# A triangular inverse on stored 64x64 diagonal chunks, each in its own corner of the array

## The chip, the cores and the metric

The kernel runs on one core of a Trainium2 chip. The metric is the device time of the whole program in microseconds. Before the change the median of three runs is 1731.29 us (1727.56 to 1732.21).

## The reference, cut to what matters

The program computes two transformer-like blocks for 256 tokens of width 1024. Only one of the four branches of the first block's mixer is touched, `rwkv7_scan`:

```python
def step(s, inp):                       # for each head, N = 64, T = 256 tokens
    r_t, w_t, k_t, v_t, a_t, b_t = inp
    sa = einsum('bhvk,bhk->bhv', s, a_t)
    s = s * w_t + sa[..., None] * b_t + v_t[..., None] * k_t
    return s, einsum('bhvk,bhk->bhv', s, r_t)
```

The kernel doesn't step through the tokens. It takes chunks of 64 tokens; within a chunk the steps depend on each other through a strictly triangular 64x64 matrix A of products of a_t and b_t, and what is needed is the inverse of (I - A), applied to the rest. There are four heads and four chunks, so 16 such matrices.

## The kernel before

The stage is one `nc.Block()` in which each engine runs its own written-out list, ordered by semaphores. Its parts, in TensorE's order from L866 on:

- **Pair products** (L870 to L879). A pair of heads' rows and a pair of chunks is one index m of 8: `pair(m)` gives the head, its channel block c, the partition half p (0 or 64, set by `odd = m // 4`) and the token block tt of 128 tokens. For each m, five kinds of 128x128 products of the scaled vectors (a·b, b·a, k·a, b·r, k·r) are made from 64 partitions each; all kinds of `odd = 0` come first, then those of `odd = 1`. Four m fill a PSUM bank; ten banks' worth go through six banks, so the later ones wait for `pair_read`. A 128x128 product spans two chunks, of which only the two diagonal 64x64 blocks are used: DVE's masks (`level0`, `levels_t`, `upper`, `upper_eq`) put zeros elsewhere.
- DVE (L666 to L683) masks them into X, XT (the inverse as built so far and its transpose), MT, MTak, MTrb, MTrk, each 8 matrices of 128x128.
- **Levels** (L881 to L899, five of them, `LEVELS`). Each doubles the size of the inverted diagonal blocks. NT is MT masked for the level (DVE, L689). TensorE makes Z = NT·X (L888), ACT copies it out of PSUM (L770, L771), TensorE makes the two products of Z with XT (L896, L897; in the last level only L897), and DVE's `grow` (L566 to L573) adds them to X and XT.
- **Gate products** (`gate_products`, L231 with `channels`): projections of the mixer's gates, with no relation to the inverse, 128x256 moving, 8 weights each, which TensorE does between the steps while DVE or ACT work. Their weights come over SP's queue through four ring slots; ACT reads the results (L542).
- **After the levels**: the MTak products (L903), DVE's copy (L695), G and H (L910), ACT's copy (L778, L779), then the products within a chunk (L918 to L920), the products per chunk (L928 to L930), a walk over the four chunks (L938, L943), and a group norm (L947, L950).

`turn` (L517) makes TensorE wait for its own last product where it goes from one half of the array's rows to the other on the same banks. Every f32 product shows as two weight loads and two matmuls in the profile.

Of the kernel before, what the change touches and what calls it, by code (L numbers as in the profile page):

```python
# [12 lines left out]
P = 128  # L13
T = 256
# [29 lines left out]
FIRST = {"lora": 512, "ln_rows": 512, "sgw": 512, "sgb": 512, "same": P, "upper": P, "upper_eq": P,  # L44
         "level0": P, "levels_t": 6 * P, "after": P, "causal": P, "sb_mask0": T, "sb_mask1": P, "carry": T,
         "eye2": 64}
# [58 lines left out]
def build(nc, out, stream, x_t, meta_t, cols, first, second, last, keep):  # L105
    with ExitStack() as ctx:
        sems = {}

        def S(name):

            if name not in sems:
                sems[name] = ctx.enter_context(nc.semaphore(name))
            return sems[name]
# [215 lines left out]
        def f(name, n=None):  # L329
            return fst[:, f_at[name]:f_at[name] + (n or FIRST[name])]  # L330
# [164 lines left out]
        X, XT, Z, NT, MT, MTak, MTrb, MTrk = (a2.take(8, P) for _ in range(8))  # L495
# [10 lines left out]
        rp, y0, yd2, state, sc_c, sc_t = X[:, 0:4, :], X[:, 4:8, :], Z[:, 0:4, :], NT[:, 0, :], y[:, 6:8, :], Z  # L506
        rp, y0, yd2 = (v.rearrange("p a b -> p (a b)").rearrange("p (c t) -> p c t", c=2) for v in (rp, y0, yd2))
# [15 lines left out]
        def four(m):  # L523
            return m.unsqueeze(1).broadcast_to([P, 4, m.shape[1]])

        def eight(m):
            return m.unsqueeze(1).broadcast_to([P, 8, m.shape[1]])

        def b3(b, w=T):

            return bank[b][:, :].rearrange("p (c t) -> p c t", t=w)
# [14 lines left out]
        with nc.Block() as block:  # L546
# [19 lines left out]
            def grow(dve, v, lev):  # L566
                dve.wait_ge(S("level_x"), lev)
                for half in range(2):
                    q4 = slice(4 * half, 4 * half + 4)
                    if lev < LEVELS:  # L570
                        vec.link(v.tensor_tensor(X[:, q4, :], X[:, q4, :], b3(4 + half, P), ALU.add))
                    ins = v.tensor_tensor(XT[:, q4, :], XT[:, q4, :], b3(6 + half, P), ALU.add)
                    vec.link(ins) if half == 0 else vec.tell(ins, S("level_grown"), lev)  # L573

            @block.vector
            def _(dve):
# [88 lines left out]
                n = 0  # L665
                lv = f("levels_t").rearrange("p (l t) -> p l t", l=6)  # L666
                for odd in range(2):
                    q4 = slice(4 * odd, 4 * odd + 4)
                    for kind in range(5):
                        b = 2 + n % 6  # L670
                        dve.wait_ge(S("pair_done"), n + 1)
                        src = b3(b, P)
                        if kind == 0:
                            vec.tell(v.tensor_tensor(X[:, q4, :], src, four(f("level0")), ALU.mult), S("pair_read"), n + 1)
                            vec.link(v.tensor_tensor(X[:, q4, :], X[:, q4, :], four(ident), ALU.add))
                        elif kind == 1:
                            vec.tell(v.tensor_copy(MT[:, q4, :], src), S("pair_read"), n + 1)
                            vec.link(v.tensor_tensor(XT[:, q4, :], MT[:, q4, :], four(lv[:, 0, :]), ALU.mult))
                            vec.link(v.tensor_tensor(XT[:, q4, :], XT[:, q4, :], four(ident), ALU.add))
                        else:  # L680
                            dst, m = ((MTak, "upper"), (MTrb, "upper_eq"), (MTrk, "upper_eq"))[kind - 2]
                            vec.tell(v.tensor_tensor(dst[:, q4, :], src, four(f(m)), ALU.mult), S("pair_read"), n + 1)
                        n += 1  # L683


                for lev in range(1, LEVELS + 1):
                    if lev > 1:
                        dve.wait_ge(S("level_z"), lev - 1)
                    vec.tell(v.tensor_tensor(NT, MT, eight(lv[:, lev, :]), ALU.mult), S("level_nt"), lev)  # L689
                    if lev > 1:  # L690
                        grow(dve, v, lev - 1)
# [37 lines left out]
            def _(act):  # L729
# [58 lines left out]
            def _(pe):  # L788
# [79 lines left out]
                n = 0  # L868
                for odd in range(2):
                    for lhs, rhs in ((a_t, b_t), (b_t, a_t), (k_t, a_t), (b_t, r_t), (k_t, r_t)):  # L870
                        if n >= 6:
                            pe.wait_ge(S("pair_read"), n - 5)
                        for m in range(4):
                            _, c, p, tt = pair(4 * odd + m)
                            o = slice(tt * P, (tt + 1) * P)
                            ins = mm(bank[2 + n % 6][:, m * P:(m + 1) * P], lhs[p:p + 64, c, o], rhs[p:p + 64, c, o],
                                     start=True, stop=True)
                        ins.then_inc(S("pair_done"), 1)
                        n += 1  # L879
                gate_products(pe, 1)  # L880
                for lev in range(1, LEVELS + 1):  # L881
                    pe.wait_ge(S("level_nt"), lev)
                    if lev == 1:
                        pe.wait_ge(S("pair_read"), 10)
# [7 lines left out]
                    pe.wait_ge(S("level_zc"), lev)  # L892
                    for m in range(8):
# [5 lines left out]
                    gate_products(pe, 1)  # L899

                for m in range(8):
                    hh, _, _, tt = pair(m)
                    ins = mm(bank[2][:, m * 64:(m + 1) * 64], MTak[:, m, :],  # L903
                             tm[:, 3, tt, hh * 64:(hh + 1) * 64], start=True, stop=True)
# [4 lines left out]
                for m in range(8):  # L909
                    ins = mm(bank[3 + m // 4][:, m % 4 * P:(m % 4 + 1) * P], XT[:, m, :], AM[:, m, :],  # L910
                             start=True, stop=True)
# [3 lines left out]
                for m in range(8):  # L915
                    hh, c, p, tt = pair(m)
                    o = slice(c * T + tt * P, c * T + (tt + 1) * P)
                    mm(bank[5][p:p + 64, o], GH[:, m, 0:64], MTrb[:, m, :], start=True, stop=True)  # L918
                    mm(bank[6][p:p + 64, o], GH[:, m, 64:P], MTrb[:, m, :], start=True, stop=False)
                    mm(bank[6][p:p + 64, o], tm[:, 3, tt, hh * 64:(hh + 1) * 64], MTrk[:, m, :], start=False, stop=True)  # L920
# [1806 lines left out]
def lay_out(a):  # L2727
# [73 lines left out]
    masks += levels[:1] + [m.T for m in levels]  # L2801
    masks += [s_ > t_, s_ <= t_, s_ < t2, s_ < t2[:, P:] - P, (t2 % 64 != 0) & (s_ >= 0)]
    eye2 = np.concatenate([np.eye(64), np.eye(64)], 0)
    first = [lora, ln_rows, sgw, sgb.reshape(P, 512)] + [m.astype(f32) for m in masks] + [eye2]
# [45 lines left out]
```

## Time and profile before

| | before |
|---|---|
| median of runs | 1731.29 us |
| profiled execution, its own time | 1728.11 us |
| its span | 1726.3 us |
| TensorE busy | 1657.2 us (96%) |
| DVE busy | 1151.3 us (67%) |
| ACT busy | 795.1 us (46%) |
| TensorE's mean granted clock | 0.984 |

The chain that ended last covers only the final few microseconds, so the profile is read by stretches. In the table of stretches and in the timeline, PE is TensorE's matmuls, PEld its weight loads. A matmul's record includes the latency from its start to its results, so consecutive records overlap; spacing is taken from starts.

### The profile page before, as it was taken

How to read it: one execution, taken by the hardware profiler on the slowest of the kernel's cores; microseconds unless marked ns; L12 is line 12 of the kernel's file. 1: busy time of each engine (PE TensorE's matmuls, PEld its weight loads, DVE VectorE, ACT ScalarE, POOL GpSimd, SP SyncE). 2: the span in 40 equal slices, each digit the busy share in tenths (PEclk: the TensorE clock that was granted, in tenths of full speed). 3: DMA queues.
4: the chain of work that ended last, by engine and by line, in shares of the span. 5: the costliest groups of instructions: out<-in, count | busy, mean ns of one | idle time of the engine just before them, and what ended most of it. 6: DMA issues, size and time to landing. Idle time of an engine off the chain costs nothing. (4 is left out here: it accounts for less than half of the span.)

```text
span 1726.3 us, 32696 instructions
## 1 busy us (share of the span) xinstructions
PE 1657.2 (96%) x11202; PEld 1508.7 (87%) x11202; DVE 1151.3 (67%) x2276; ACT 795.1 (46%) x1318; POOL 354.3 (21%) x225
## 2 busy tenths in 40 slices
PE   7999998979999999999999998999999999999997
PEld 7988897869999977778999998999999888888886
DVE  6473414667777584662779994777776577777776
ACT  5251112245554363223455554455555555555554
POOL 1030000014443001335767995000000000000000
PEclk9999998989999999999999999999999999999999
DMA  7423223335555521115545786555556877777773
GB/s 280 146 61 110 74 86 135 99 125 188 186 183 185 181 64 50 49 47 184 196 150 188 219 228 182 181 178 171 178 172 199 240 239 237 235 235 241 242 238 127
DMA packets 92806, 289.47 MB, mean 168 GB/s; under 512 B 10304, under 2 KB 27072, under 8 KB 92352
## 3 DMA queue, kind: packets, MB, share of 16 engines
q1 hardware_dynamic: 92304, 287.61, 51.8%
q10 hardware_dynamic: 432, 0.90, 0.2%
q8 instruction: 47, 0.77, 0.2%
q14 instruction: 23, 0.19, 0.0%
HBM read 270.64 MB, written 17.83 MB: 167 GB/s over the span
## 5 line engine op out<-in xcount | busy, mean ns | idle before, releaser
L260 PE MATMUL psum<-arena_parts 128*128 128x256 f32 (+2 forms) x1664 | 478.9, 288 | 24.9 <-DVE ring_parts L255 11.8
L262 PE MATMUL psum<-arena_parts,ring_parts 128*128 128x256 f32 (+1 forms) x1600 | 450.8, 282 | 0.0
L2638 DVE TENSOR_TENSOR ring_parts<-ring,arena_parts 128x512 fp32r<-128x512 f32 x418 | 282.6, 689 | 113.2 <-ACT arena_parts L2438 94.5
L260 PEld LDWEIGHTS psum<-arena_parts 128*128 128x128 f32 x1664 | 316.0, 190 | 27.8 <-DVE ring_parts L255 10.9
L262 PEld LDWEIGHTS psum<-arena_parts,ring_parts 128*128 128x128 f32 x1600 | 304.2, 190 | 0.0
L261 PE MATMUL psum<-h_parts,arena_parts 128*128 128x256 f32 x1024 | 290.2, 283 | 0.0
L255 POOL TENSOR_TENSOR ring_parts<-ring,arena_parts 128x1024 fp32r<-128x1024 f32 x79 | 211.0, 2695 | 64.7 <-ACT arena_parts L251 47.8
L231 PE MATMUL psum<-h,ring 128*128 128x256 f32 x896 | 210.4, 394 | 0.0
L2407 PE MATMUL psum<-arena_parts,x_parts 128*128 128x512 f32 x512 | 198.8, 388 | 2.7 <-DVE x_parts L2665 2.7
L2409 PE MATMUL psum<-arena_parts,x_parts 128*128 128x512 f32 x512 | 201.2, 393 | 0.0
L2408 PE MATMUL psum<-ring_parts,x_parts 128*128 128x512 f32 x512 | 200.9, 392 | 0.0
L231 PEld LDWEIGHTS psum<-h,ring 128*128 128x128 f32 x896 | 174.6, 198 | 28.5 <-issue 3.2
L261 PEld LDWEIGHTS psum<-h_parts,arena_parts 128*128 128x128 f32 x1024 | 194.1, 190 | 0.0
L2438 ACT ACTIVATE arena_parts<-ring 128x512 fp32r<-128x512 f32 x209 | 131.5, 629 | 112.0 <-PE psum L2409 93.1
L261 PE MATMUL psum<-arena_parts 128*128 128x256 f32 (+1 forms) x576 | 163.6, 284 | 0.0
L2435 ACT ACTIVATE arena_parts<-ring 128x512 fp32r<-128x512 f32 x209 | 131.8, 631 | 67.1 <-PE psum L2409 55.4
L1108 DVE TENSOR_TENSOR ring_parts<-ring,arena_parts 128x1024 fp32r<-128x1024 f32 x66 | 84.3, 1284 | 52.8 <-ACT arena_parts L1103 48.2
L2407 PEld LDWEIGHTS psum<-arena_parts,x_parts 128*128 128x128 f32 x512 | 96.1, 188 | 24.8 <-DVE ring_parts L2638 2.9
L2408 PEld LDWEIGHTS psum<-ring_parts,x_parts 128*128 128x128 f32 x512 | 96.1, 188 | 22.0
L2409 PEld LDWEIGHTS psum<-arena_parts,x_parts 128*128 128x128 f32 x512 | 96.3, 188 | 19.1
L261 PEld LDWEIGHTS psum<-arena_parts 128*128 128x128 f32 x576 | 110.0, 191 | 0.2
L251 ACT ACTIVATE arena_parts<-ring 128x1024 fp32r<-128x1024 f32 x76 | 78.6, 1053 | 60.3 <-DMA ring<-stream 60.3
(540 smaller groups left out, 2952.9 us busy)
## 6 DMA issues: line engine op xcount, KB each, us to landing
ring<-stream SPq DMA_DIRECT2D x473, 512.0 KB, 3.6
kept<-arena SPq DMA_DIRECT2D x128, 128.0 KB, 2.0
arena<-kept SPq DMA_DIRECT2D x32, 512.0 KB, 4.1
arena<-first SPq DMA_DIRECT2D x1, 2144.0 KB, 16.5
arena<-second SPq DMA_DIRECT2D x1, 1632.0 KB, 6.4
x<-x_t SPq DMA_DIRECT2D x1, 1024.0 KB, 5.6
out<-arena SPq DMA_DIRECT2D x4, 256.0 KB, 2.1
arena<-last ACTq DMA_DIRECT2D x1, 512.0 KB, 3.5
```

Source lines behind the costliest of these rows:

```text
L231: mm = nc.tensor.matmul(b[:, 0:width], w[:, k, :], h[:, k, lo:lo + width], start=k == 0, stop=k == KT - 1)
L255: ns.tensor_tensor(low[:, s, :], ring[:, s, :], high[:, s, :].bitcast(F32), ALU.subtract)\
L260: nc.tensor.matmul(dst, stationary[0], moving[0], start=first, stop=False)
L261: nc.tensor.matmul(dst, stationary[0], moving[1], start=False, stop=False)
L262: return nc.tensor.matmul(dst, stationary[1], moving[0], start=False, stop=last_one)
L1108: nc.vector.tensor_tensor(low[:, s, :], ring[:, s, :], high[:, s, :].bitcast(F32), ALU.subtract)\
L2407: mm(b, gate_high[:, q % 4, t], expert_high[:, m % 2, w], start=False, stop=False)
L2408: mm(b, gate_high[:, q % 4, t], low[:, s, w], start=False, stop=False)
L2409: ins = mm(b, gate_low[:, q % 4, t], expert_high[:, m % 2, w], start=False, stop=last_one)
L2435: nc.scalar.activation(expert_high[:, m % 2, halves[0]], ring[:, s, halves[0]], ACT.Copy)\
L2438: nc.scalar.activation(expert_high[:, m % 2, halves[1]], ring[:, s, halves[1]], ACT.Copy)\
L2638: v.tensor_tensor(low[:, s, w], ring[:, s, w], expert_high[:, m % 2, w].bitcast(F32), ALU.subtract)\
```

## The change

X, XT, Z, NT, MT, MTak, MTrb and MTrk are stored as 8 matrices of 64 columns: partitions 0 to 63 hold the first chunk's 64x64 block, 64 to 127 the second's. All masks are stacked in the same way on the host, with a zero pad so that `first` has its old size. Each 128x128 product of the inverse becomes two 64x64 products, one from and to rows 0 to 63, the other from and to rows 64 to 127. The pair products run in the order kind, m, chunk r, `odd`, so that successive ones alternate the row halves; they fit in six banks at once, and DVE reads two banks in one operation. The X and XT additions, NT and the copy of Z are one operation of 512 elements per partition each. The products within a chunk (`within`) alternate the two heads' column halves, and are done for one row half at a time, before the chunk products of the same half. y0 has its own place. Added waits: `pair_read` 4 before the first product with Z, `pair_read` 6 before the MTak products.

```diff
-        X, XT, Z, NT, MT, MTak, MTrb, MTrk = (a2.take(8, P) for _ in range(8))
+        X, XT, Z, NT, MT, MTak, MTrb, MTrk = (a2.take(8, CH) for _ in range(8))
+        y0 = a2.take(2, T)
...
-                for half in range(2):
-                    q4 = slice(4 * half, 4 * half + 4)
-                    if lev < LEVELS:
-                        vec.link(v.tensor_tensor(X[:, q4, :], X[:, q4, :], b3(4 + half, P), ALU.add))
-                    ins = v.tensor_tensor(XT[:, q4, :], XT[:, q4, :], b3(6 + half, P), ALU.add)
-                    vec.link(ins) if half == 0 else vec.tell(ins, S("level_grown"), lev)
+                if lev < LEVELS:
+                    vec.link(v.tensor_tensor(X, X, b3(3, CH), ALU.add))
+                vec.tell(v.tensor_tensor(XT, XT, b3(7, CH), ALU.add), S("level_grown"), lev)
...
+                dve.wait_ge(S("pair_done"), 1)
+                vec.tell(v.tensor_tensor(by_half(X), pairs_of(2, 0), each(f("level0")), ALU.mult), S("pair_read"), 1)
+                vec.tell(v.tensor_copy(by_half(MT), pairs_of(2, 1)), S("pair_read"), 2)
+                vec.link(v.tensor_tensor(X, X, eight(f("eye2")), ALU.add))
+                vec.tell(v.tensor_tensor(NT, MT, eight(lv[:, 1, :]), ALU.mult), S("level_nt"), 1)
+                vec.link(v.tensor_tensor(XT, MT, eight(lv[:, 0, :]), ALU.mult))
+                vec.tell(v.tensor_tensor(XT, XT, eight(f("eye2")), ALU.add), S("pair_read"), 3)
+                for kind, (dst, b, half, m) in enumerate(((MTrk, 6, 0, "upper_eq"), (MTak, 4, 0, "upper"), (MTrb, 4, 1, "upper_eq"))):
+                    dve.wait_ge(S("pair_done"), 3)
+                    vec.tell(v.tensor_tensor(by_half(dst), pairs_of(b, half), each(f(m)), ALU.mult), S("pair_read"), 4 + kind)
...
-                    a.activation(Z[:, 0:4, :], b3(2, P), ACT.Copy)
-                    sca.tell(a.activation(Z[:, 4:8, :], b3(3, P), ACT.Copy), S("level_zc"), lev)
+                    sca.tell(a.activation(Z, b3(2, CH), ACT.Copy), S("level_zc"), lev)
...
+                for kind, (lhs, rhs) in enumerate(((a_t, b_t), (b_t, a_t), (k_t, a_t), (b_t, r_t), (k_t, r_t))):
+                    for m in range(4):
+                        for r in range(2):
+                            for odd in range(2):
+                                _, c, p, tt = pair(4 * odd + m)
+                                o = slice(tt * P + CH * r, tt * P + CH * (r + 1))
+                                at_m = kind % 2 * T + m * CH
+                                ins = mm(bank[2 + kind // 2 * 2 + odd][chunk_rows[r], at_m:at_m + CH],
+                                         lhs[p:p + 64, c, o], rhs[p:p + 64, c, o], start=True, stop=True)
+                    if kind % 2 or kind == 4:
                         ins.then_inc(S("pair_done"), 1)
...
                     for m in range(8):
-                        ins = mm(bank[2 + m // 4][:, m % 4 * P:(m % 4 + 1) * P], NT[:, m, :], X[:, m, :],
-                                 start=True, stop=True)
+                        for r in chunk_rows:
+                            ins = mm(bank[2][r, m * CH:(m + 1) * CH], NT[r, m, :], X[r, m, :], start=True, stop=True)
...
                     for m in range(8):
-                        o = slice(m % 4 * P, (m % 4 + 1) * P)
+                        o = slice(m * CH, (m + 1) * CH)
                         if lev < LEVELS:
-                            mm(bank[4 + m // 4][:, o], XT[:, m, :], Z[:, m, :], start=True, stop=True)
-                        ins = mm(bank[6 + m // 4][:, o], Z[:, m, :], XT[:, m, :], start=True, stop=True)
+                            for r in chunk_rows:
+                                mm(bank[3][r, o], XT[r, m, :], Z[r, m, :], start=True, stop=True)
+                        for r in chunk_rows:
+                            ins = mm(bank[7][r, o], Z[r, m, :], XT[r, m, :], start=True, stop=True)
...
                 for m in range(8):
-                    ins = mm(bank[3 + m // 4][:, m % 4 * P:(m % 4 + 1) * P], XT[:, m, :], AM[:, m, :],
-                             start=True, stop=True)
+                    for r in chunk_rows:
+                        ins = mm(bank[3 + m // 4][r, m % 4 * P:(m % 4 + 1) * P], XT[r, m, :], AM[r, m, :],
+                                 start=True, stop=True)
...
+                def within(r):
+                    for m in range(4):
+                        two_heads = [(4 * odd + m, *pair(4 * odd + m)) for odd in range(2)]
+                        for j, hh, c, p, tt in two_heads:
+                            o = slice(c * T + tt * P + r.start, c * T + tt * P + r.stop)
+                            mm(bank[5][p:p + 64, o], GH[r, j, 0:64], MTrb[r, j, :], start=True, stop=True)
...
                 for ch in (0, 2, 1, 3):
                     if ch == 1:
                         turn(pe, ins)
+                    if ch < 2:
+                        within(chunk_rows[ch])
```

## Rows read from the trace of the kernel before

**Rows 1.** The page: the span, and engines' busy time with its share of the span.

```profile
span 1726.3 us, 32696 instructions
PE 1657.2 (96%) x11202; PEld 1508.7 (87%) x11202; DVE 1151.3 (67%) x2276; ACT 795.1 (46%) x1318; POOL 354.3 (21%) x225
```

**Rows 2.** Stretches: us; PE, PEld, DVE, ACT, POOL busy (instructions); clock, DMA share, GB/s.

```profile
165.89:174.68 8.79, 8.79 (x82) 8.67 (x81) 7.18 (x11) 0.47 (x1) 0.00 (x0) 1.00 0.18 60
174.68:180.04 5.36, 3.72 (x17) 2.96 (x16) 5.10 (x7) 0.47 (x1) 0.00 (x0) 1.00 0.10 9
180.04:192.20 12.16, 12.16 (x80) 11.36 (x81) 3.97 (x5) 1.56 (x3) 0.00 (x0) 1.00 0.25 84
192.20:204.47 12.27, 12.27 (x82) 11.44 (x81) 3.97 (x5) 2.04 (x4) 0.00 (x0) 1.00 0.30 87
...
229.00:239.48 10.48, 10.48 (x66) 9.65 (x65) 1.37 (x2) 2.04 (x4) 0.00 (x0) 1.00 0.28 102
239.48:244.24 4.76, 3.86 (x34) 3.73 (x33) 0.69 (x1) 1.08 (x3) 0.00 (x0) 1.00 0.35 110
...
251.35:256.35 5.00, 5.00 (x49) 4.83 (x48) 0.00 (x0) 0.47 (x1) 0.00 (x0) 1.00 0.33 108
256.35:259.90 3.55, 3.49 (x98) 3.29 (x97) 0.00 (x0) 0.00 (x0) 0.00 (x0) 1.00 0.00 0
...
270.45:290.45 20.00, 14.88 (x77) 10.13 (x77) 10.05 (x14) 3.55 (x6) 0.00 (x0) 0.74 0.06 26
```

**Rows 3.** Timeline, pair stage: start, us, engine, line, operation, tiles, count [idle before].

```profile
165.89 8.86 PE L876 MATMUL psum<-arena 64*128 64x128 f32 x80
...
167.16 0.69 DVE L674 TENSOR_TENSOR arena<-psum,arena 128x512 f32<-128x512 f32 x1 [24.06 <-PE psum L876]
...
176.59 2.14 DVE L682 TENSOR_TENSOR arena<-psum,arena 128x512 f32<-128x512 f32 x3
...
178.76 1.23 DVE L689 TENSOR_TENSOR arena<-arena 128x1024 f32<-128x1024 f32 x1
...
180.04 2.05 PE L888 MATMUL psum<-arena 128*128 128x128 f32 x16 [1.64 <-DVE arena L689]
```

**Rows 4.** Timeline of one level, the second.

```profile
192.41 1.95 PE L888 MATMUL psum<-arena 128*128 128x128 f32 x16
...
194.20 3.62 PE L231 MATMUL psum<-h,ring 128*128 128x256 f32 x16
...
203.66 0.69 DVE L572 TENSOR_TENSOR arena<-arena,psum 128x512 f32<-128x512 f32 x1
```

**Rows 5.** Timeline, the walk over chunks: products on the two diagonal corners.

```profile
270.45 0.31 PEld L938 LDWEIGHTS psum<-arena 64*64 64x64 f32 x8 [0.33 <-issue]
...
270.74 0.40 PE L943 MATMUL psum<-arena 64*64 64x64 f32 x8
```

**Rows 6.** Timeline: the second half of the chunk products, and the column-halved L844.

```profile
136.89 1.15 PE L844 MATMUL psum<-arena 128*64 128x128 f32 x16
...
258.19 0.19 PEld L928 LDWEIGHTS psum<-arena 64*64 64x64 f32 x2 [0.20 <-PE psum L930]
...
259.69 0.28 PE L930 MATMUL psum<-arena 64*64 64x64 f32 x2
```

**Rows 7.** Timeline of L815 to L817, where the tile's size changes.

```profile
113.17 0.18 PEld L815 LDWEIGHTS psum<-arena 64*128 64x128 f32 x1 [0.33 <-issue]
...
113.49 0.38 PE L815 MATMUL psum<-arena 64*128 64x256 f32 x1
...
113.80 0.30 PEld L817 LDWEIGHTS psum<-arena 128*128 128x128 f32 x2 [0.33 <-issue]
```

**Rows 8.** Timeline after the levels: MTak products, copy, G and H, gate products.

```profile
239.69 1.89 PE L903 MATMUL psum<-arena 128*128 128x64 f32 x16
...
241.69 0.69 DVE L695 COPY arena<-psum 128x512 f32<-128x512 f32 x1 [3.78 <-PE psum L903]
242.49 2.02 PE L910 MATMUL psum<-arena 128*128 128x128 f32 x16 [0.90 <-issue]
...
244.35 7.07 PE L231 MATMUL psum<-h,ring 128*128 128x256 f32 x32
```

More of the change, by code:

```diff
@@ L42 @@
         "ssm_log_dt_2": 16, "ml_b_if_2": 2}
-FIRST = {"lora": 512, "ln_rows": 512, "sgw": 512, "sgb": 512, "same": P, "upper": P, "upper_eq": P,
-         "level0": P, "levels_t": 6 * P, "after": P, "causal": P, "sb_mask0": T, "sb_mask1": P, "carry": T,
-         "eye2": 64}
+CH = 64
+FIRST = {"lora": 512, "ln_rows": 512, "sgw": 512, "sgb": 512, "same": P, "upper": CH, "upper_eq": CH,
+         "level0": CH, "levels_t": 6 * CH, "after": P, "causal": P, "sb_mask0": T, "sb_mask1": P, "carry": T,
+         "eye2": 64, "unused": 9 * CH}
 SECOND = {"b_re": 512, "b_im": 512, "c_re": 512, "c_im": 512, "w_if": 192, "neg0": T, "neg1": T, "sel": 512}
@@ L527, in eight, with pairs_of, by_half, each @@
             return m.unsqueeze(1).broadcast_to([P, 8, m.shape[1]])
+        def pairs_of(b, kind):
+            two = psum[:, b * 512:(b + 2) * 512].rearrange("p (o x) -> p o x", o=2)
+            return two[:, :, kind * T:(kind + 1) * T].rearrange("p o (m k) -> p o m k", k=CH)
+        def by_half(m):
+            return m.rearrange("p (o m) k -> p o m k", o=2)
+        def each(m):
+            return m.unsqueeze(1).unsqueeze(1).broadcast_to([P, 2, 4, CH])
         def b3(b, w=T):
@@ L662, in _ @@
                 vec.tell(v.tensor_copy(y[:, 2:4, :], b3(3)), S("early_read"))
-                n = 0
                 lv = f("levels_t").rearrange("p (l t) -> p l t", l=6)
[L667 to L683, printed above, removed]
@@ new lines, in _ @@
+                vec.link(v.tensor_tensor(XT, MT, eight(lv[:, 0, :]), ALU.mult))
[3 more added lines that the diff above has]
+                    vec.tell(v.tensor_tensor(by_half(dst), pairs_of(b, half), each(f(m)), ALU.mult), S("pair_read"), 4 + kind)
+                for lev in range(2, LEVELS + 1):
+                    dve.wait_ge(S("level_z"), lev - 1)
@@ L867, in _ @@
                 pe.wait_ge(S("tm_read"), 1)
[L868 to L876, printed above, removed]
-                                     start=True, stop=True)
+                chunk_rows = [slice(CH * r, CH * (r + 1)) for r in range(2)]
+                for kind, (lhs, rhs) in enumerate(((a_t, b_t), (b_t, a_t), (k_t, a_t), (b_t, r_t), (k_t, r_t))):
[8 more added lines that the diff above has]
+                    if kind % 2 or kind == 4:
                         ins.then_inc(S("pair_done"), 1)
-                        n += 1
                 gate_products(pe, 1)
@@ L883, in _ @@
                     if lev == 1:
-                        pe.wait_ge(S("pair_read"), 10)
+                        pe.wait_ge(S("pair_read"), 2)
                     else:
@@ L892, in _ @@
                     pe.wait_ge(S("level_zc"), lev)
+                    if lev == 1:
+                        pe.wait_ge(S("pair_read"), 4)
                     for m in range(8):
-                        o = slice(m % 4 * P, (m % 4 + 1) * P)
+                        o = slice(m * CH, (m + 1) * CH)
                         if lev < LEVELS:
-                            mm(bank[4 + m // 4][:, o], XT[:, m, :], Z[:, m, :], start=True, stop=True)
-                        ins = mm(bank[6 + m // 4][:, o], Z[:, m, :], XT[:, m, :], start=True, stop=True)
+                            for r in chunk_rows:
+                                mm(bank[3][r, o], XT[r, m, :], Z[r, m, :], start=True, stop=True)
+                        for r in chunk_rows:
+                            ins = mm(bank[7][r, o], Z[r, m, :], XT[r, m, :], start=True, stop=True)
                     ins.then_inc(S("level_x"), 1)
                     gate_products(pe, 1)
+                pe.wait_ge(S("pair_read"), 6)
                 for m in range(8):
                     hh, _, _, tt = pair(m)
-                    ins = mm(bank[2][:, m * 64:(m + 1) * 64], MTak[:, m, :],
-                             tm[:, 3, tt, hh * 64:(hh + 1) * 64], start=True, stop=True)
+                    for r in chunk_rows:
+                        ins = mm(bank[2][r, m * 64:(m + 1) * 64], MTak[r, m, :],
+                                 tm[r, 3, tt, hh * 64:(hh + 1) * 64], start=True, stop=True)
                 ins.then_inc(S("mv_done"), 1)
@@ L909, in _ @@
                 for m in range(8):
-                    ins = mm(bank[3 + m // 4][:, m % 4 * P:(m % 4 + 1) * P], XT[:, m, :], AM[:, m, :],
-                             start=True, stop=True)
+                    for r in chunk_rows:
+                        ins = mm(bank[3 + m // 4][r, m % 4 * P:(m % 4 + 1) * P], XT[r, m, :], AM[r, m, :],
+                                 start=True, stop=True)
                 ins.then_inc(S("gh_done"), 1)
@@ L914, in _ @@
                 pe.wait_ge(S("gh_read"), 1)
[L915 to L920, printed above, removed]
+                def within(r):
[4 more added lines that the diff above has]
+                            mm(bank[5][p:p + 64, o], GH[r, j, 0:64], MTrb[r, j, :], start=True, stop=True)
+                        for j, hh, c, p, tt in two_heads:
+                            o = slice(c * T + tt * P + r.start, c * T + tt * P + r.stop)
+                            mm(bank[6][p:p + 64, o], GH[r, j, 64:P], MTrb[r, j, :], start=True, stop=False)
+                        for j, hh, c, p, tt in two_heads:
+                            o = slice(c * T + tt * P + r.start, c * T + tt * P + r.stop)
+                            mm(bank[6][p:p + 64, o], tm[r, 3, tt, hh * 64:(hh + 1) * 64], MTrk[r, j, :], start=False, stop=True)
                 for ch in (0, 2, 1, 3):
@@ L2801, in lay_out @@
     masks += levels[:1] + [m.T for m in levels]
+    masks[1:] = [np.concatenate([m[:CH, :CH], m[CH:, CH:]], 0) for m in masks[1:]]
     masks += [s_ > t_, s_ <= t_, s_ < t2, s_ < t2[:, P:] - P, (t2 % 64 != 0) & (s_ >= 0)]
     eye2 = np.concatenate([np.eye(64), np.eye(64)], 0)
-    first = [lora, ln_rows, sgw, sgb.reshape(P, 512)] + [m.astype(f32) for m in masks] + [eye2]
+    first = [lora, ln_rows, sgw, sgb.reshape(P, 512)] + [m.astype(f32) for m in masks] + [eye2, np.zeros((P, 9 * CH))]
     first = np.concatenate([x.astype(f32, copy=False) for x in first], 1)
```

10 lines of the change are left out of this document (3 added, 7 removed).

## The prediction

> **What bounds the kernel now.** I read the page first: TensorE is busy for 1657.2 of the span's 1726.3 us, 96%, and every other engine is far below it [rows 1]. That says where to look, not what this change is worth, so the next view is the table of stretches, cut at the starts of the stage's pieces [rows 2]. The changed code runs from 165.89 us (the pair products) to 259.90 us (the last chunk product). In the four rounds of the levels, and in the products of L918 to L920, TensorE has no idle time at all; it waits only in 174.68 to 180.04 (busy 3.72 of 5.36 us) and in 239.48 to 244.24 (3.86 of 4.76). DVE has 4 of 12.27 us of work in a level, ACT 2, and DMA is below 0.36 of its capacity in all these stretches. So here time is what TensorE has to stream, plus two waits for DVE.
>
> The third view is the timeline. In the pair stage TensorE is done by 174.7, but DVE's 16 masking operations, started at 167.16, end at 178.7 (0.72 us each), then comes NT (1.23 us), and the first level starts only at 180.04 [rows 3]. In a level the order is products of NT and X, a gate product, products with Z, a gate product. DVE's last addition ends at 204.35, when the second gate product is just being finished [rows 4]: the two engines are balanced, with TensorE ahead by nothing.
>
> A word on units. Each f32 product is two passes (a weight load and a matmul each); "pass" below is one of them. A full 128x128 pass with 128 moving columns takes 0.112 us (16 of L888 take 1.79 us, from 192.41 to 194.20 [rows 4]). A gate product takes 3.45 us: 32 passes last 7.07 us and 16 last 3.62 [rows 4, 8], the difference. Check: 2 x 3.45 + 48 x 0.112 = 12.28, and a level lasts 12.27 [rows 2].
>
> **The pace of 64x64 passes.** The change makes two passes on a 64x64 tile out of each 128x128 pass, the two in different corners of the array. It pays only if corners run at the same time. The nearest rows are L938 and L943, whose tiles are just these two diagonal corners, and which write the two row halves of one PSUM bank, as the new levels do: 16 passes, weights from 270.45, last matmul record until 271.14, which holds about 0.1 us of first load and 0.17 us of latency (a 256-column record lasts 0.38 us for 0.21 us of columns [rows 7]). That leaves 0.42 us for 16, 0.026 us each [rows 5]. L928 to L930 alternate two corners of one row half: from 258.29 to 259.80, 48 passes, 0.031 us each, and over the whole stretch with its turn 3.55/98 = 0.036 [rows 2, 6]. I take 0.028 and keep 0.026 and 0.031 as ends. With 128 moving columns on two corners I take 0.056, since L844 (two column halves) does 16 in 1.15 us, 0.058 apart [rows 6].
>
> **The price of changing the tile's size.** From L815 (64x128) to L817 (128x128) and between them the records show it: weights of L815 at 113.17, of L817 at 113.80, 0.63 us for two passes of 256 columns, which need 0.43 [rows 7]. (L816 runs beside them on the other row half.) So each change of size costs 0.2 us. Before, a level has none; after it has four, 0.84 us with rounding upward. Bounds: 0.1 (the weight load alone) and 0.33 us (the idle time that the profile gives the load queue there).
>
> **Part by part.**
> Pair products: 80 passes become 160, and now all four corners are used in turn. At 0.028 they take 4.5 us; no row shows four corners at once, so the bounds are 0.015 (twice two corners) and 0.031, that is 2.4 and 5.0 us. I stay at the two-corner pace, the nearest row. The Trainium skill ("TensorE: Matmul & The Clock Gate", its section on the clock's levels and floors) says that matmuls never start less than about 25 ns apart, however few the columns; by that rule the four corners would give 4.0 us and not 2.4. No row here has a burst under 0.026, which agrees. DVE now gets its first data after 64 passes, not 8; 165.99 + 1.8 + 0.3 = 168.1 (0.3 as today, from 8 x 0.108 past 165.99 to 167.16), and needs four operations before level 1 may start (X masked, MT, X plus identity, NT, each 512 wide, 4 x 0.72): 171.0. TensorE does its passes until 170.5, changes size (0.2), does a gate product (3.45), changes again (0.2): 174.35. The gate product thus covers DVE by 3.3 us; were it absent, level 1 would wait for DVE until 171.0. Today's first matmul of level 1 is at 180.04 plus 0.1 of load. Gain 5.8 us (5.3 to 7.9). The remaining five DVE operations end at about 174.7, and the added wait (MTrk read before the first Z product, because bank 7 is reused) ends at 173.2; the Z product is due at 174.35 + 0.9 + 3.85 = 179.1, so nothing queued behind it on TensorE is held.
>
> Levels 1 to 4: 2 x 3.45 + 96 x 0.028 + 0.84 = 10.43 against 12.27 (12.16 in the first). Gain 4 x 1.84 - 0.1 = 7.25 us (6.1 with 0.031, 10 with 0.026 and 0.1 us switches). DVE's part shrinks with it: NT 1.23 to 0.69, four additions to two, so 1.45 us after a Z product, under the 3.45 of the gate product; ACT's copy of Z is one operation, not two. Neither becomes late. Level 5 has no product for X: 6.9 + 64 x 0.028 + 0.84 = 9.53 against 10.48, gain 0.95.
>
> MTak products and G/H: today 4.66 us from the first matmul at 239.69 to the gate's at 244.35. Of this 2.0 are passes until DVE's copy starts at 241.69, 0.8 the copy and the wait for it (L910 at 242.49), 1.86 the L910 passes [rows 8]. After: 0.2 + 0.9 + 0.2 + 0.8 + 32 x 0.056 + 0.2 = 4.1. Gain 0.5: the wait stays, and 128 moving columns on two corners only break even.
>
> L918 to L920: 48 passes of a 128x64 tile with 128 columns take 5.0 us, because the two column halves stand in two long blocks. They become 96 alternating passes, 2.7 us plus 0.1; the switch to 64x64 before L928 goes too. Gain 2.2 us (1.9 to 2.4). The moved turn between row halves costs its 0.2 us once as before.
>
> The rest has one answer: the `first` transfer keeps its size by a zero pad, y0 gets a place of its own, the masks are the same elements stacked. The loads on SP's queue wait for the slots as before and only come some us earlier; DMA has room [rows 2]. After 259.90 the stage ends with an alternation of DVE and TensorE, and then a block boundary at which all engines meet, so the gain is passed on whole.
>
> Sum: 5.8 + 7.25 + 0.95 + 0.5 + 2.2 = 16.7 us, within 14 to 21. The profiled execution is 1728.11 us (span 1726.3), so it would come to 1711.4; the median of the runs, 1731.29, to **1714.6 us**. A measurement of this kernel tells about 0.3% (5.2 us) from no change.
>
> **The rivals.**
> (a) Corners of different row halves do not run together when they write the same bank. Then a 64x64 pass costs 0.056 (half of 0.112, since L903, with 64 moving columns but full weights, is no faster than 0.118 and so is bound by the weight's columns [rows 8]). A level takes 6.9 + 5.4 + 0.84 = 13.1, a loss of 3.5 over four; level 5 loses 0.85; MTak and G/H (3.6 for the latter) 2.1; pairs (a bank for each row half) and L918 (one row half at a time) keep their 8.0. Net gain 1.5 us: 1729.8, no change. The Trainium skill ("TensorEngine Tiling (Array Packing)", on PSUM pressure) states just this rule. Against it stand L938 and L943, which are two row halves on one bank at 0.026. Chance 6%.
> (b) The clock. TensorE's granted clock is 1.00 through the whole stage and falls to a mean of 0.74 in 270.45 to 290.45, where it waits again and again [rows 2]. If short passes on half the array drew the 1.2 GHz level in turns, at the same mean 0.74, the 66 us from the pairs to the second gate product after G/H would take 89, 23 more: 6.5 us slower than today, 1737.8. It decides from a mean clock of 66/(66+16.7) = 0.80 downward. Against it: the clock is 1.00 in 256.35 to 259.90, which is 64x64 passes alone. Chance 4%.
> (c) The passes come slower, at the 0.036 of the whole L928 stretch, because TensorE has to be fed 768 more instructions. Pairs then gain 4.5, levels 4.2, level 5 0.4, the next 0.2, L918 1.4: 10.7 us, 1720.6. Chance 12%.
> (d) Four corners at once and cheaper switches: 20 us, 1711. Chance 13%.
> That the change does not do what it says shows as a level with 48 passes; the text of the diff leaves no room for it.
>
> **How the numbers follow.** The forecast (gain 14 to 19) has 65%. Range: from 1705 (the best bounds, 21 us, plus some 4 us of spread between runs and of where the clock falls in the 20 us after the stage) to 1723 (case c, and 2.5 us of spread). It leaves out (a), (b) and little else, some 15%. Chances: faster by over 0.3%: 0.89; same: 0.07; slower: 0.04.
>
> **What would show it.** A level's period of 10.4 us (12.3 would show the 0.028 or the switches wrong); z bursts of 32 passes in 0.9 us; level 1 starting 8.4 us after the first pair product instead of 14.1, with no idle time before it; L918 to L920 in 2.7 us; granted clock 1.00 up to G/H; the stage from the first pair product to the first gate product after the chunk products 77 us instead of 94. Wrong is the forecast if two diagonal corners take 0.056 a pass, or if gate products in the stage last longer than 3.45.

## The result, and the profile after

The changed kernel takes 1714.46 us in the median of five runs (1702.33 to 1714.53), against 1731.29 for the kernel before (five runs, 1727.56 to 1732.65). The ratio is 0.9891, with a 95% interval of 0.9857 to 0.9925. The forecast was 1714.6 us. That the two agree to 0.2 us is partly luck, as shown below: the stage gained 19.4 us, not the 16.7 of the sum.

The profiled execution of the changed kernel is its fastest, 1702.33 us. The page opens with its span and busy times:

```profile
span 1700.5 us, 33437 instructions
PE 1632.5 (96%) x11586; PEld 1484.7 (87%) x11586; DVE 1136.4 (67%) x2259; ACT 792.9 (47%) x1313; POOL 355.0 (21%) x225
```

TensorE has 384 more passes and 25 us less busy time. Of this difference only a part is the change's, as the next section shows. The stretches that answer to rows 2, with the same columns, are: pairs until level 1; the second level; MTak products to G and H; the products within a chunk and per chunk; and the whole stage from the first pair product to the first gate product after the chunk products.

```profile
164.66:170.81 6.15, 6.15 (x178) 5.39 (x177) 4.64 (x7) 0.47 (x1) 0.00 (x0) 1.00 0.31 88
181.20:191.59 10.39, 10.39 (x130) 8.87 (x129) 2.06 (x3) 1.54 (x3) 0.00 (x0) 1.00 0.33 103
221.83:225.78 3.95, 3.04 (x65) 2.76 (x64) 0.69 (x1) 1.08 (x3) 0.00 (x0) 1.00 0.44 137
232.88:239.24 6.36, 6.30 (x194) 6.09 (x193) 0.00 (x0) 0.47 (x1) 0.00 (x0) 1.00 0.31 85
164.66:239.24 74.58, 73.61 (x1074) 63.65 (x1073) 15.87 (x23) 11.31 (x23) 0.00 (x0) 1.00 0.33 100
```

And the whole stage in the kernel before, in the same view:

```profile
165.89:259.89 94.00, 91.40 (x689) 84.79 (x688) 30.24 (x40) 13.77 (x28) 0.00 (x0) 1.00 0.25 79
```

The stage went from 94.00 to 74.58 us. The granted clock is 1.00 in every piece. TensorE's idle time at the start of level 1 is gone; the one between MTak products and G and H is left. The timeline of the changed kernel (start, duration, engine, line, operation, count) shows the pair stage:

```profile
164.66 2.56 PE L876 MATMUL psum<-arena 64*64 64x64 f32 x160
...
165.96 0.69 DVE L678 TENSOR_TENSOR arena<-psum,arena 128x512 f32<-128x512 f32 x1 [23.39 <-PE psum L876]
167.15 3.32 PEld L233 LDWEIGHTS psum<-h,ring 128*128 128x128 f32 x16
167.15 3.72 PE L233 MATMUL psum<-h,ring 128*128 128x256 f32 x16
...
168.14 0.69 DVE L681 TENSOR_TENSOR arena<-arena 128x512 f32<-128x512 f32 x1
...
170.32 2.14 DVE L686 TENSOR_TENSOR arena<-psum,arena 128x512 f32<-128x512 f32 x3
...
170.81 1.15 PE L889 MATMUL psum<-arena 64*64 64x64 f32 x32
```

160 pair passes are done in 2.56 us; the one gate product follows and then level 1, without a wait. NT (L681), which level 1 needs, is DVE's fourth operation and ends at 168.83, 2 us before. In rows 3 the same point was reached 14.15 us after the first pair product, here after 6.15. One Z burst (L889) has 32 passes in 1.15 us; in rows 4 it was 16 passes in 1.95.

Piece by piece, before minus after, from the starts in the two traces:

| piece | before | after | gain | forecast |
|---|---|---|---|---|
| first pair product to level 1 | 14.15 | 6.15 | 8.0 | 5.8 |
| levels 1 to 4 | 48.96 | 41.56 | 7.4 | 7.25 |
| level 5 | 10.48 | 9.46 | 1.0 | 0.95 |
| MTak products to the gate after G and H | 4.76 | 3.95 | 0.8 | 0.5 |
| two gate products | 7.11 | 7.10 | 0.0 | 0 |
| L918 to the end of the chunk products | 8.55 | 6.36 | 2.2 | 2.2 |
| sum | 94.0 | 74.6 | 19.4 | 16.7 |

### The profile page after: what moved, and what is told of

The parts are those of the page before. It is cut to its first block and busy times, and to the rows that moved or that the text cites. A ratio compares the mean times of both kernels' runs of the same rounds, so it can differ in the third digit from the quotient of the medians.

```text
span 1700.5 us, 33437 instructions
## 1 busy us (share of the span) xinstructions
PE 1632.5 (96%) x11586; PEld 1484.7 (87%) x11586; DVE 1136.4 (67%) x2259; ACT 792.9 (47%) x1313; POOL 355.0 (21%) x225
## 5 line engine op out<-in xcount | busy, mean ns | idle before, releaser
L233 PE MATMUL psum<-h,ring 128*128 128x256 f32 x896 | 205.5, 387 | 0.0
L233 PEld LDWEIGHTS psum<-h,ring 128*128 128x128 f32 x896 | 170.1, 193 | 26.9 <-issue 2.5
## 6 DMA issues: line engine op xcount, KB each, us to landing
arena<-first SPq DMA_DIRECT2D x1, 2144.0 KB, 16.7
```

The costliest lines, as they stand in the source:

```text
L233: mm = nc.tensor.matmul(b[:, 0:width], w[:, k, :], h[:, k, lo:lo + width], start=k == 0, stop=k == KT - 1)
```

## The experiments

### The same two kernels again: is 19.4 us the change's worth?

> The changed kernel, unaltered. Its profiled execution was at 1702.33 us, the other four at 1713.2 to 1714.5. Theory C (the clock): the rest of the difference to the kernel before, past the 19.4 us that the stage itself lost, is how long TensorE's granted clock stood at its lower level, which differs from execution to execution; the stage itself is again 74.6 us long from the first pair product to the first gate product after the chunk products, and a profiled execution near 1714 shows about 20 us more at 0.5 than the 34 us of the 1702 one. Rival: the 12 us lie in the changed stage or in a transfer; then a stretch at full clock differs in length.

> The kernel before, unaltered, for a second profile. Theory C: the stage lasts 94.0 us again from the first pair product to the first gate product after the chunk products, to 0.1 us, and what differs from the first profile's 1728.11 us lies outside it, where the granted clock stands at its lower level for another length than the 58 us of the first. Rival: the stage itself varies by some us, and then the 19.4 us read from two profiles is not the change's worth.

The changed kernel had a median of 1714.08 us (six runs, 1711.63 to 1718.07), the kernel before 1733.31 (eleven runs, 1724.98 to 1738.41): ratio 0.9895, interval 0.9868 to 0.9923. The second profiles were of executions at 1716.59 us (changed) and 1732.72 us (before). The stage in them, changed kernel first, then the kernel before:

```profile
165.93:240.50 74.57, 73.61 (x1073) 63.66 (x1072) 15.88 (x23) 11.32 (x23) 0.00 (x0) 1.00 0.33 100
```

```profile
164.52:258.52 94.00, 91.41 (x689) 84.82 (x688) 30.25 (x40) 13.75 (x28) 0.00 (x0) 1.00 0.26 79
```

The stage repeats to 0.01 us in both kernels, so 19.4 us is what the change takes out of it. What differs between the two executions of the changed kernel, 14.3 us, lies outside. A large part is the granted clock behind stages in which TensorE waits. The stretch from the end of the stage to the first product of the next one, in the 1702 us execution and then in the 1717 us one, shows it:

```profile
239.24:266.45 27.21, 21.52 (x126) 17.11 (x125) 13.10 (x19) 4.47 (x8) 0.00 (x0) 1.00 0.27 97
```

```profile
240.50:270.05 29.55, 24.47 (x126) 18.93 (x125) 13.11 (x19) 4.45 (x8) 0.00 (x0) 0.88 0.24 90
```

The same 126 matmuls take 2.3 us longer at a mean clock of 0.88. Summed over stretches of 2 us, the clock stands at its lower level for 39 us in the one execution and 62 us in the other (the expectation had 34 for the first and some 20 more for the second). But 23 us at half speed can cost at most 11 or 12, not 14.3. The rest was not expected: in the last part of the program, at a clock of 1.00, the same loop runs 1% slower. Here are 50 us of it in the 1702 us and the 1717 us execution:

```profile
1500.00:1550.00 50.00, 50.00 (x220) 41.05 (x219) 37.55 (x75) 28.65 (x55) 0.00 (x0) 1.00 0.72 234
```

```profile
1500.00:1550.00 50.00, 50.00 (x218) 40.55 (x218) 37.03 (x72) 28.37 (x55) 0.00 (x0) 1.00 0.70 231
```

220 matmuls against 218. The kernel before has both paces too: 220 in the profile at 1728.11 us, 218 in the one at 1732.72, and from the first to the last product of the loop it takes 351.0 us in the one and 354.4 in the other. In the changed kernel these are 351.0 and 356.0 us; some 1.7 us of the difference are 3.4 us at the lower clock at the loop's start, and the other 3.3 the pace. Theory C holds for the stage and for what the clock can explain of the changed kernel's spread. For the kernel before its second half failed: the lower clock lasts 56 us in both of its profiles, and most of the 4.6 us between them is the pace of that loop. So a stretch at full clock does differ in length, as the rival of the first expectation had it, but not in the changed stage; what sets the pace stays open.

So a difference of two profiles is no measure of this change (25.8 us for the first pair of profiles, 16.1 for the second), but the length of the stage is.

### What makes the corners run together

The pair products use all four corners, and their pace was the largest miss of the sum. Three kernels change only the order of the same 160 passes. First, all passes of one kind on one row half, then those of the other:

```diff
-                    for m in range(4):
-                        for r in range(2):
-                            for odd in range(2):
+                    for odd in range(2):
+                        for m in range(4):
+                            for r in range(2):
```

> The pair products of each kind in the order row half, m, chunk: 16 passes on the two corners of one row half, then 16 on those of the other. Theory R (it takes alternating row halves to have four corners at once): two corners at 0.028, the 160 passes take 4.5 us instead of 2.5 and level 1 starts 2.0 us later. Rival Q (TensorE's queue reaches ahead and fills all corners in any order): 2.5 us as now.

Then corner by corner within a kind:

```diff
+                    for r in range(2):
+                        for odd in range(2):
+                            for m in range(4):
```

> The pair products of each kind corner by corner, 8 passes in each. Theory R: one corner at a time, 0.056 a pass, 9.0 us; level 1 then starts 6.5 us later than in the changed kernel. Rival Q: 2.5 us. In between (blocks of 8 overlap in part): 4.5 to 5.

And all kinds on one row half before any on the other (`for odd` outside `for kind`):

> All 80 pair passes on one row half first, then the 80 of the other, chunks alternating: never more than two corners in use but at the one seam. At the pace of two corners, 0.028, 4.5 us. With blocks of 16 passes for each row half (tried before) it was 3.3 us, 0.019 a pass: if that was blocks overlapping at their seams, this is 4.4 to 4.5; if two column halves alone reach 0.019, it is 3.1.

The timelines, in this order, of L876 in the three kernels:

```profile
166.03 3.33 PE L876 MATMUL psum<-arena 64*64 64x64 f32 x160
```

```profile
167.65 6.14 PE L876 MATMUL psum<-arena 64*64 64x64 f32 x160
```

```profile
164.34 4.71 PE L876 MATMUL psum<-arena 64*64 64x64 f32 x160
```

A record's length holds 0.22 us for the last pass; from start to start the mean spacing is (2.56 - 0.22)/159 = 0.0147 us in the changed kernel, 0.0196 in blocks of 16 per row half, 0.0282 with two corners throughout, 0.0372 in blocks of 8 per corner. Two corners give the 0.028 that the prediction took, and four corners in turn run about twice as fast. Level 1 starts 6.15, 6.91, 8.29 and 9.72 us after the first pair product: what the passes lose is lost whole, since nothing else in that piece waits. Neither theory was right in full: the blocks per row half were expected at 4.5 or 2.5 us and took 3.33, those by corner at 9.0, 2.5 or some 4.5 to 5 between them, and took 6.14. Of the two forecasts for two corners throughout, the one in which blocks overlap at their seams (4.4 to 4.5 us) held, with 4.5.

The seams can be counted. If a pass costs 0.058 us on one corner (measured in the next run) and 0.028 on two, the blocks by corner save 159 x 0.058 - 5.92 = 3.3 us over 19 seams, the blocks per row half 159 x 0.028 - 3.11 = 1.3 us over 9. Both come to 0.15 to 0.17 us a seam, some three passes of one corner. These are estimates from the spacings above; by them a block overlaps with the next only at its end, whatever its length, and one seam in 160 passes is too little to be seen.

The same for the level products, each chunk's eight matrices in a block:

```diff
-                    for m in range(8):
-                        for r in chunk_rows:
+                    for r in chunk_rows:
+                        for m in range(8):
                             ins = mm(bank[2][r, m * CH:(m + 1) * CH], NT[r, m, :], X[r, m, :], start=True, stop=True)
...
-                        if lev < LEVELS:
-                            for r in chunk_rows:
-                                mm(bank[3][r, o], XT[r, m, :], Z[r, m, :], start=True, stop=True)
-                        for r in chunk_rows:
-                            ins = mm(bank[7][r, o], Z[r, m, :], XT[r, m, :], start=True, stop=True)
+                    for r in chunk_rows:
+                        for m in range(8):
+                            o = slice(m * CH, (m + 1) * CH)
+                            if lev < LEVELS:
+                                mm(bank[3][r, o], XT[r, m, :], Z[r, m, :], start=True, stop=True)
+                            ins = mm(bank[7][r, o], Z[r, m, :], XT[r, m, :], start=True, stop=True)
```

> The level products run all 8 matrices of the first chunk's corner, then all 8 of the second's (blocks of 16 passes in Z, of 32 in the products with Z; 16 in the last level). The pair products showed 0.037 us a pass for blocks of 8 and 0.014 with alternation. Theory R (overlap comes from neighbours in the order, a block's end at most): nearly 0.056 a pass, a level of 10.4 + 96 x 0.022 to 0.028 = 12.5 to 13.1 us, longer than in the kernel before. Rival Q (TensorE's queue fills both corners in any order): 10.4.

```profile
183.40 1.90 PE L889 MATMUL psum<-arena 64*64 64x64 f32 x32
185.22 3.72 PE L233 MATMUL psum<-h,ring 128*128 128x256 f32 x16
...
190.44 0.28 PE L900 MATMUL psum<-arena 64*64 64x64 f32 x2
190.56 0.33 PE L899 MATMUL psum<-arena 64*64 64x64 f32 x4
190.67 0.33 PE L900 MATMUL psum<-arena 64*64 64x64 f32 x4
190.84 0.28 PE L899 MATMUL psum<-arena 64*64 64x64 f32 x2
...
196.22 1.90 PE L889 MATMUL psum<-arena 64*64 64x64 f32 x32
```

A level lasts 196.22 - 183.40 = 12.82 us, 0.55 longer than in the kernel before (12.27, rows 2), and the whole execution 1722.36 us. Theory R held here. The 96 passes cost 2.43 us more than alternated, so about 0.053 each instead of 0.028. The lines of L899 and L900 show why it is no more: within a block two passes start every 0.117 us (190.44 to 190.56), 0.058 each, but where the two blocks of the products with Z meet, eight start in 0.28 us (190.56 to 190.84) instead of 0.47. That is one seam, read directly. Half-size storage alone, with its changes of the tile's size, would have made the levels slower than the full products; the gain is the neighbours' overlap. This also refutes rival (a): the alternated passes are on one bank, in different row halves, and do run two at a time.

### What a change of the tile's size costs

```diff
                     ins.then_inc(S("level_z"), 1)
-                    gate_products(pe, 1)
...
                     ins.then_inc(S("level_x"), 1)
-                    gate_products(pe, 1)
+                    gate_products(pe, 2)
```

> Both gate products of a level stand behind the products with Z, none between Z and these. Two changes of the tile's size go (0.2 us each), and TensorE waits for ACT's copy of Z instead: latency 0.2, copy 0.6, latency 0.1 and the first load, about 1.0 us. If a change costs 0.2 us, a level lasts 10.4 - 0.4 + 1.0 = 11.0 us; if it costs 0.33, 10.7; if it costs nothing, 11.4. The wait could also draw the lower clock; then single levels last longer.

```profile
170.70 1.15 PE L889 MATMUL psum<-arena 64*64 64x64 f32 x32
...
172.55 0.33 PE L898 MATMUL psum<-arena 64*64 64x64 f32 x4 [0.70 <-ACT arena L771]
...
174.56 7.17 PE L233 MATMUL psum<-h,ring 128*128 128x256 f32 x32
...
181.66 1.15 PE L889 MATMUL psum<-arena 64*64 64x64 f32 x32
```

A level lasts 10.96 us, against 10.39 with a gate product in between: 11.0 was expected for 0.2 us a change. It can be read directly: two gate products and the change to 64x64 take 181.66 - 174.56 = 7.10 us; one gate product and the change take 3.65 in the changed kernel:

```profile
171.88 3.72 PE L233 MATMUL psum<-h,ring 128*128 128x256 f32 x16
...
175.53 0.33 PE L899 MATMUL psum<-arena 64*64 64x64 f32 x4
...
175.70 0.28 PE L901 MATMUL psum<-arena 64*64 64x64 f32 x4
...
177.33 0.28 PE L901 MATMUL psum<-arena 64*64 64x64 f32 x4
...
177.55 3.72 PE L233 MATMUL psum<-h,ring 128*128 128x256 f32 x16
```

The difference is a gate product, 3.45, and what is left, for the change from 128x128 to 64x64, is 0.20. The change back is nearer 0.15: 56 passes from 175.70 to 177.33 start 0.029 us apart, so of the 3.09 us of a level that are not gate products and changes to 64x64 the 96 passes take 2.8, and the two changes back share 0.3. The wait for ACT costs about 0.9 to 1.0 us, so a gate product in it pays although it brings two changes. The clock stayed at 1.00 up to the end of the stage.

### The orders alone, in the kernel before

```diff
-                for odd in range(2):
-                    for lhs, rhs in ((a_t, b_t), (b_t, a_t), (k_t, a_t), (b_t, r_t), (k_t, r_t)):
+                for kind, (lhs, rhs) in enumerate(((a_t, b_t), (b_t, a_t), (k_t, a_t), (b_t, r_t), (k_t, r_t))):
...
                         for m in range(4):
-                            _, c, p, tt = pair(4 * odd + m)
+                            for odd in range(2):
+                                _, c, p, tt = pair(4 * odd + m)
...
                 pe.wait_ge(S("gh_read"), 1)
-                for m in range(8):
+                for m in (0, 4, 1, 5, 2, 6, 3, 7):
```

DVE's loop takes kinds outside and `odd` inside to match.

> The kernel before, with its 128x128 storage, but the pair products alternate the row halves (64x128 tiles, kinds in the outer loop) and the products within a chunk alternate the column halves. Nothing else changes. Theory D (in the pair stage DVE's 16 operations set the time, in the levels TensorE's passes): the 80 pair passes take 4.5 to 5 us instead of 8.9 and level 1 starts no earlier than now (14.1 us after the first pair product), levels stay at 12.27, the L918 to L920 products take 2.8 us instead of 5.0. In all 2.2 us. Rival (the order alone brings the pair stage's gain): level 1 starts 4 us earlier, 6 us in all.

```profile
164.56 2.95 PE L875 MATMUL psum<-arena 64*128 64x128 f32 x48
168.04 1.16 PE L875 MATMUL psum<-arena 64*128 64x128 f32 x16 [0.53 <-DVE arena L674]
171.67 1.16 PE L875 MATMUL psum<-arena 64*128 64x128 f32 x16 [2.47 <-DVE arena L677]
172.76 5.41 PE L231 MATMUL psum<-h,ring 128*128 128x256 f32 x16
178.73 2.05 PE L886 MATMUL psum<-arena 128*128 128x128 f32 x16 [0.56 <-DVE arena L689]
```

Theory D held. The passes themselves run at 0.058 instead of 0.108, but TensorE then waits for DVE to free banks, and level 1 starts 14.17 us after the first pair product, as before. The levels stay at 12.27. The L918 to L920 products gain 2.0 us, by their order alone. In all the stage is 92.06 us, 1.9 of the 19.4. The one execution took 1728.21 us.

The pair stage's 8.0 us came because DVE got out of the way: it has 9 operations there instead of 17 (NT counted in both), and only four of them stand ahead of level 1, where all 17 did; the faster passes are worth something only behind that.

These are two changes in one. The half-size tiles halve the operations; that NT now comes before the masks of MTak, MTrb and MTrk is an order, which the kernel before might have had too. With its full-size tiles X, X plus identity, MT and NT would be six operations of 0.72 us and one of 1.23, 5.6 us instead of the 12.8 from 165.84 to the end of NT at 178.67. No run takes that order alone, so what each of the two is worth is not shown. An estimate from these rows: MT would be out of its banks at 170.2, the last 16 pair passes (1.1 us) and the gate product (3.45) would follow, and level 1 would start near 174.9 instead of 178.73, about half of the 8.0 us. (The two masks of MTrb, whose banks level 1 writes, would be done by 172.9.)

The view of stretches shows a side effect of TensorE's waits here:

```profile
172.76:178.73 5.97, 5.41 (x18) 4.14 (x17) 5.68 (x8) 0.47 (x1) 0.00 (x0) 0.71 0.01 3
```

After its two waits TensorE was granted the lower clock for some 3.5 us, and the gate product, 3.72 us elsewhere, lasted 5.41. It did no harm only because DVE was later still.

### A version with the remaining waits filled

One gate product moves from behind G and H to behind the MTak products, one from behind the chunk products to behind the first step over the chunks, one to between the two group norm products:

```diff
                 ins.then_inc(S("mv_done"), 1)
+                gate_products(pe, 1)
...
                 ins.then_inc(S("gh_done"), 1)
-                gate_products(pe, 2)
+                gate_products(pe, 1)
...
                 ins.then_inc(S("chunk_ops"), 1)
-                gate_products(pe, 3)
+                gate_products(pe, 1)
...
                     ins.then_inc(S("state_step"), 1)
+                    if ch == 1:
+                        gate_products(pe, 1)
...
                     .then_inc(S("gn_mean"), 1)
+                gate_products(pe, 1)
```

> One of the two gate products after G/H goes between the MTak products and G/H, one of the three after the chunk products between the first and second step over the chunks, one between the two group norm products. Waits of 0.9, 0.8 and 1.6 us are covered, and two of the three places cost two more changes of the tile's size (0.4 us each): 2.5 us less. Where those waits also drew the lower clock behind the stage (3 to 10 us at 0.5 in earlier profiles), up to 5 us more. Rival: the end of the stage is set by DVE's chain after the second group norm product, so a gate product ahead of it only delays that: 1.8 us slower.

It takes 1707.13 us in the median of six runs (1701.9 to 1708.62), 0.9846 of the kernel before (interval 0.9818 to 0.9875), against 1714.08 for the changed kernel beside it on the same chip. Its tail in the timeline:

```profile
242.18 0.45 PE L956 MATMUL psum<-arena 64*64 64x64 f32 x8
242.46 0.40 PE L961 MATMUL psum<-arena 64*64 64x64 f32 x8
242.79 3.72 PE L233 MATMUL psum<-h,ring 128*128 128x256 f32 x16
246.44 0.45 PE L956 MATMUL psum<-arena 64*64 64x64 f32 x8
...
249.08 1.13 PE L967 MATMUL psum<-arena 128*128 128x512 f32 x2 [0.73 <-DVE arena L712]
250.05 3.62 PE L233 MATMUL psum<-h,ring 128*128 128x256 f32 x16
```

The stage is 73.79 us, 0.8 less; the stretch behind it is 24.66 us, against 27.21 in the changed kernel's profile without clock loss there and 29.55 in the one with it. So 3.3 us come from the waits themselves (2.5 expected), and the rest of the 7 us is, in this profile, clock that was not lost: 1.00 in that stretch, and 48 us at the lower level in the whole execution. One profile of a varying quantity doesn't show that the clock gain is lasting, but all six runs are below all six of the changed kernel beside them (in the first set one execution of the changed kernel, at 1702.33 us, was as fast). The rival (DVE's chain sets the end) fell.

## Why the prediction was right, and where its steps were off

- **What bounds the stage** (TensorE's passes in the levels, DVE in the pair stage) held: `levels_by_chunk` lengthens a level by what its passes lose, and `old_orders_alternated` starts level 1 no earlier with faster passes.
- **The pace on two corners**, 0.028, held in the levels (0.029 between starts; 10.39 us, 10.43 forecast), in L918 to L920, and in the experiment with two corners throughout (0.0282). Its rows were L938 and L943 [rows 5], of the same shape and place; that nearness is why it held.
- **The pace on four corners** was the mis-sized term: 0.028 taken, 0.0147 measured, 2.2 of the 2.7 us missing in the sum. It lay at the far bound of the prediction (0.015). No row of before showed four corners, and I took the nearest row rather than twice it. The rule of the Trainium skill quoted there ("TensorE: Matmul & The Clock Gate", "Wait — 56ns, not 53.3ns?"), that matmuls never start less than about 25 ns apart, is contradicted by 14.7 ns over 160 passes. By it the passes would have taken 4.0 us, and the gain would still have come out too small.
- **The change of size**, 0.2 us, held towards 64x64 (0.20); back to 128x128 it is nearer 0.15. **DVE's cover** held: its fourth operation ended at 168.83, the gate product gave way to level 1 at 170.81.
- **MTak to G and H**: 0.8 instead of 0.5. Most of that is bookkeeping: the sum has the change of size ahead of MTak twice, once among the four of level 5 and once here (0.2), and it starts the old piece at its first matmul, 239.69, where the table starts it at the first weight load (4.66 against 4.76 us). G and H were 0.1 us faster than the sum (1.89 from 223.89 to 225.78, with the change), and the MTak products with the wait behind them 0.15 slower (1.26 from 221.83 to DVE's copy at 223.09).
- **Rival (a)**, row halves on one bank, fell: 32 passes in 1.15 us on one bank. With it fell, for these tiles, the rule of the Trainium skill ("TensorEngine Tiling (Array Packing)", "Gotcha 1: PSUM Pressure") that names the same limit. (In its price, L903's passes are 0.111 us apart by their starts, 1.89 less 0.22 over 15, and not 0.118; this changes nothing in it.) **Rival (b)**, the clock in the stage, fell: 1.00 in all profiles of the changed kernel there. **Rival (c)** fell: 320 instructions of the pair products were issued in 2.5 us, so feeding TensorE was no limit. **Rival (d)** was half right: four corners at once, but hardly cheaper switches.
- **The total** hit more closely than the sum, because the medians differ by 16.8 us in one set of runs and by 19.2 in the other. The spread outside the stage (clock, last loop) is wider than the miss.

## What to carry to other kernels

A product that uses only diagonal blocks of the array gains from being cut only if the pieces alternate corners in the order written: 0.058 us a pass on one corner fell to 0.028 on two and 0.015 on four, while the levels with the pieces in long blocks were 0.55 us longer than with the uncut product, changes of size included. Look first at what waits behind the products: where DVE's evacuation sets the time, a better order on TensorE alone brought nothing, and half-size tiles on DVE together with making first what the next step needs brought 8 us. Each change between 64x64 and 128x128 tiles costs 0.15 to 0.2 us, less than a wait of 1 us that the work in between covers.

## What the runs showed of the hardware that was not expected

- Matmuls of 64x64 tiles with 64 moving columns start 0.0147 us apart on average when four corners alternate, weight loads included.
- Where a block of passes on one corner (or one row half) meets the next, the two overlap for a few passes only, some 0.15 us a seam: eight passes in 0.28 us at the seam in `levels_by_chunk`, and 0.037 and 0.020 us a pass in blocks of 8 and 16 of the pair products. With one seam in 160 passes the pace is that within the block, 0.028.
- The same program spent 39 us in one execution and 62 in another at the lower granted clock, mostly behind stretches with waits. It isn't always a wait: in the 1702 us execution the clock fell at 712.4 us, although TensorE had been busy for 7.94 of the 8 us before; from 707.5 to 711.4 us these were passes on 32 columns or 32 rows of the array. Separately, a loop of 128x512 matmuls at clock 1.00 ran at 220 or at 218 matmuls per 50 us, in both kernels; its cause is open.
